# Output projections: squares added up on VectorE before TensorE sums them

## The reference, cut to what matters

```python
def rms_norm(x, gain):
    y = x * lax.rsqrt(jnp.mean(x * x, axis=-1, keepdims=True) + NORM_EPS)
    return y * gain

# first block, after the attention branches
x = x + rms_norm(merged @ w_out, mix_post_norm)

# each of the two layers of the second block
x = x + g1 * (mixed @ w_out_2)
h2 = modulate(rms_norm(x, ffn_norm_g_2), sh2, sc2)
x = x + g2 * hierarchical_moe(h2, ...)     # router, then 32 experts
```

## Time and profile before

| | |
|---|---|
| median of the runs | 1594.91 us |
| the profiled execution, its own time | 1594.11 us |
| its span in the profile | 1592.4 us |
| TensorE busy | 1458.5 us (92%) |
| VectorE busy | 903.3 us (57%) |
| ScalarE busy | 576.6 us (36%) |
| mean TensorE clock granted, share of full | 0.961 |
| read from HBM | 416.71 MB |

### The profile page before, as it was taken

How to read it: one execution, slowest core, us unless ns; L and a number is a source line. 1 busy time by engine, 2 the same in 40 slices (tenths; PEclk the granted TensorE clock), 3 DMA queues, 4 the chain that set the end, 5 groups by cost and what they waited for, 6 DMA issues and landing times.

```text
span 1592.4 us, 27000 instructions
## 1 busy us (share of the span) xinstructions
PE 1458.5 (92%) x10609; PEld 1180.4 (74%) x10609; DVE 903.3 (57%) x1609; ACT 576.6 (36%) x916; POOL 3.7 (0%) x9
## 2 busy tenths in 40 slices
PE   9999999989888899999999999987779999988776
PEld 8999999979787898999989898422217989532223
DVE  6898877684444476888877985210015996410002
ACT  4544356423435544433445153221115143321101
POOL 0000000000000000000000000000000000000000
PEclk9999999999989998999999999999988999999897
DMA  8998844412513353988866558899996749699995
GB/s 304 381 356 306 307 166 154 148 43 107 186 67 107 106 167 138 339 308 305 301 225 220 190 207 323 332 409 409 409 409 234 280 133 373 266 408 409 409 409 222
DMA packets 115804, 420.88 MB, mean 264 GB/s; under 512 B 12944, under 2 KB 13088, under 8 KB 115568
## 3 DMA queue, kind: packets, MB, share of 16 engines
q1 hardware_dynamic: 114624, 414.19, 69.8%
q0 software_dynamic: 1072, 5.20, 0.9%
HBM read 416.71 MB, written 2.62 MB: 263 GB/s over the span
## 4 chain that ended last, share of the span: by engine, by line
PE 68%; DMA 11%; SPq 7%; DVE 6%; ACT 4%; issue 3%; DVEq 0%; ACTq 0%
PE work L930 26%; PE acc L930 12%; PE work L965 7%; SPq L752 7%; PE work L1021 5%; PE work L1566 3%; DMA hf<-wstream_d 3%; PE work L890 2%; PE work L900 2%; DMA over_splits<-wstream_d 2%; ACT whi L1656 2%; PE work L1593 1%; DVE wlo L2106 1%; PE work L1501 1%; DMA over_select<-wstream_d 1%
## 5 line engine op out<-in xcount | busy, mean ns | idle before, releaser
L2106 DVE TENSOR_TENSOR wlo<-raw,whi 128x1024 fp32r<-128x1024 f32 x264 | 320.9, 1222 | 176.6 <-ACT whi L1656 176.0
L1656 ACT ACTIVATE whi<-raw 128x1024 fp32r<-128x1024 f32 x264 | 277.0, 1056 | 280.3 <-PE work L930 191.7
L930 PE MATMUL work<-hhi,whi 128*128 128x256 f32 x1024 | 295.0, 288 | 1.7 <-DVE wlo L2106 0.9
L930 PE MATMUL work<-hlo,whi 128*128 128x256 f32 x1024 | 292.9, 286 | 0.0
L930 PE MATMUL work<-hhi,wlo 128*128 128x256 f32 x1024 | 292.7, 286 | 0.0
L930 PEld LDWEIGHTS work<-hhi,whi 128*128 128x128 f32 x1024 | 200.0, 195 | 3.9 <-DVE wlo L2106 3.0
L930 PEld LDWEIGHTS work<-hlo,whi 128*128 128x128 f32 x1024 | 199.9, 195 | 0.3
L930 PEld LDWEIGHTS work<-hhi,wlo 128*128 128x128 f32 x1024 | 199.7, 195 | 0.0
L2845 DVE TENSOR_TENSOR pair_b<-work,pair_a 128x256 f32<-128x256 f32 x16 | 6.8, 424 | 215.3 <-ACT pair_a L2061 215.3
L2212 DVE SCALAR_TENSOR_TENSOR ada_tiles<-ada_tiles,c_act 128x1024 f32<-128x1024 f32 x96 | 116.3, 1219 | 2.0 <-DMA ada_tiles<-ada_d 2.0
L965 PE MATMUL work<-hf,raw 128*128 128x256 f32 x512 | 111.5, 379 | 0.0
(11 more groups left out here) (482 smaller groups left out, 2708.5 us busy)
## 6 DMA issues: line engine op xcount, KB each, us to landing
raw<-wstream_d SPq DMA_DIRECT2D x376, 512.0 KB, 4.7
ada_tiles<-ada_d SPq DMA_DIRECT2D x96, 512.0 KB, 5.2
over_splits<-wstream_d SPq DMA_DIRECT2D x80, 512.0 KB, 15.3
over_select<-wstream_d SPq DMA_DIRECT2D x48, 512.0 KB, 14.5
over_end<-wstream_d SPq DMA_DIRECT2D x24, 512.0 KB, 14.9
spare_d<-wstream_d SPq DMA_DIRECT2D x24, 512.0 KB, 14.4
over_pool<-wstream_d SPq DMA_DIRECT2D x22, 512.0 KB, 15.2
hf<-wstream_d SPq DMA_DIRECT2D x20, 512.0 KB, 15.0
```

The lines of the kernel that those rows point to most:

```text
L930: mm = pe.matmul(out, a, b, start=(start and k == 0), stop=(stop and k == n - 1), skip_group_check=skip)
L1656: act.activation(whi[n % AHEAD][:], tiles[SLOT[SPLITS[n]]][:], ACT.Copy).then_inc(s("hi_done"), 1)
L2106: dve.tensor_tensor(wlo[n % AHEAD][:], tiles[SLOT[SPLITS[n]]][:], whi[n % AHEAD][:].bitcast(F32), ALU.subtract).then_inc(s("lo_done"), 1)
```

## The change

VectorE adds the squares of pair 1 and then of pair 2 onto those of pair 0, in place in `hf`, each when ScalarE has written them. The second add signals `squares_added`. TensorE leaves out the groups for pair 1 and 2: its group for pair 0 now stands behind tile 7 and waits for `squares_added`; the group for pair 3 stays last. `router_part` stays where it was, and waits for the squares of its pair by itself. In the layers one zero product instead of five stands between the two groups. The three places are the first projection (norm 4) and that of each layer (norms 9 and 12).

```diff
@@ norm_part, TensorE
-            def norm_part(k, j):
+            def norm_part(k, j, added=None):
...
-                pe.wait_ge(s("norm_sq"), NORM_AT[k] + j + 1)
+                if added is None:
+                    pe.wait_ge(s("norm_sq"), NORM_AT[k] + j + 1)
+                else:
+                    pe.wait_ge(s("squares_added"), after("squares_added", added))
@@ router_part, TensorE
+                pe.wait_ge(s("norm_sq"), NORM_AT[9 + 3 * l] + j + 1)
                 if j == 0:
@@ out_tiles, TensorE
-                    if n > 4:
-                        norm_part(k, n - 5)
-                        if layer is not None:
-                            router_part(layer, n - 5)
+                    if n > 4 and layer is not None:
+                        router_part(layer, n - 5)
+                norm_part(k, 0, 1 if layer is None else 2 + layer)
                 hold(1, hold_last)
                 norm_part(k, 3)
@@ the layers' call, TensorE
-                out_tiles(f"wout{l}", "mixed_ready", 4 * l, k + 2, 5, 0, l)
+                out_tiles(f"wout{l}", "mixed_ready", 4 * l, k + 2, 1, 0, l)
@@ VectorE
+            def add_squares(k, j):
+
+                dve.wait_ge(s("norm_sq"), NORM_AT[k] + j + 1)
+                return dve.tensor_tensor(hf[:, 0:2, :], hf[:, 0:2, :], hf[:, 2 * j:2 * j + 2, :], ALU.add)
...
             for m in range(DC - 1):
                 lo(NUMBER[START["wout"] + m] + AHEAD)
+                if m == 5:
+                    own(add_squares(4, 1))
+                elif m == 6:
+                    add_squares(4, 2).then_inc(s("squares_added"), 1)
...
                         residual_pair(m - 4, lambda m: mod_col(l, 2, m))
+                    if m == 5:
+                        own(add_squares(k + 2, 1))
+                    elif m == 6:
+                        add_squares(k + 2, 2).then_inc(s("squares_added"), 1)
```

More of the change, by code:

```diff
@@ L332 @@
     **shared("dn_vector", [(n, 1) for n in ("dn_absz", "dn_decay", "dn_var", "dn_gc", "dn_recip", "dn_rest", "dn_unit",
-                                            "dn_scales", "dn_ovar", "dn_orecip", "dn_scaled", "dn_out")]),
+                                            "dn_scales", "dn_ovar", "dn_orecip", "dn_scaled", "dn_out")]
+             + [("squares_added", 1 + LAYERS)]),
     **shared("first_scalar", [("c_ready", 1), ("mem_squares", 4), ("mem_high", 4)]),
```

## The result

The changed kernel takes 1585.35 us in the median of 8 runs (1582.43 to 1590.12), against 1594.91 for before; the measured ratio is 0.995, 95% interval 0.9935 to 0.9965. That is 8.0 us; by the two medians alone it would be 9.6. Single executions of one kernel differ by 7 to 10 us within a sample, so it matters what in the 7 to 8 us is the change's own.

The account below looks back on a forecast made before the run. It took TensorE's path (68% of the chain) as the bound, with DMA at 18%. From the profiled 1594.11, less 1.07 and 2 x 2.45, plus 1.67 for clock, came 1589.81; adding 0.80 for the median gave 1590.6, range 1588.3 to 1593.1.

Parts of the forecast that it names:

- Sums removed, layers: Each layer's output projection: two groups of sums of 0.79 us go, saving 1.58; with the zero products 2.45.
- Zero products: Between the layers' last sums: five become one, saving 0.87 us a layer, with 0.35 us of slack left.
- First projection: Two groups removed save 1.58 us, less a 0.51 wait for VectorE's add: a gain of 1.07.
- Work in sum: First projection's 1.07 us plus 2.45 in each of two layers: 5.97 saved before any clock cost.
- Expert stages: Transfers start when TensorE frees the first buffer, so a gain ahead of the stage survives as an earlier start.
- The rival falls: Rival: transfer-bound expert stages swallow the layers' gain, leaving only the first projection's 1.07 us; 1593.8, chance 0.10.
- The clock: TensorE's clock falls behind the sums in one of the two layers, costing 1.67 us; chance 0.38.
- rival "slower": Clock lost behind both layers' sums through zero products and gather: 4.11 us a layer plus 0.71; 1597.9, chance 0.04.
- The row of 617 to 618: Profile slice by the first projection's sums: TensorE busy 1.00 while its clock falls, taken as evidence busy time can cost clock.
- the reading that only idleness costs clock: Reading of the skill's clock-gate page: no idle time added in the layers, so no clock cost; sum 1588.95.
- the case without any fall: Rival: no clock is lost in the layers; 1588.9 us, or 1588.2 if layer 0's gather keeps its clock; chance 0.28.

Follow-up runs that it names:

- adds first, one: Changed kernel with VectorE's adds ahead of the splits in the first projection, one zero product per layer kept; ratio 0.995 (0.9935 to 0.9965).
- with none: Changed kernel with no zero product between the two groups of sums in the layers; ratio 0.9972 (0.9957 to 0.9987).
- the second profile of the change: Changed kernel run once more, unaltered, for a second sample of executions; ratio 0.9956 (0.9942 to 0.9969), median 1587.49 us.
- one, alone: Kernel before with one zero product in place of five in each layer, nothing else; ratio 0.9972 (0.9959 to 0.9985).
- layers only: Changed kernel with the first projection put back to four groups of sums, only both layers changed; ratio 0.9988 (0.9974 to 1.0002).

## Why the prediction was wrong, step by step

- *Sums removed, layers.* Right in kind, slightly small. Forecast 2.45 a layer with the zero products, shown 2.66 (12.90 to 10.24): each of the three router groups behind a tile is 0.10 shorter, which no row of before showed, and the sums with the zero product are 0.09 longer.
- *Zero products.* Right: 0.87 a layer (12.90 to 12.03 alone, 11.11 to 10.24 in the change). The cover was as thin as computed: in "adds first, one" the last squares end 0.34 before their sum, where 0.35 was forecast, and with none nothing more is won.
- *First projection.* The mechanism was right: the add behind the split, done at 613.31 against 613.25. Forecast 1.07, shown 0.88 at full clock (12.22 to 11.34) and 0.29 where the clock falls in the sums. The tiles close up by 1.79, not 1.58 (first to last squares 10.42 before, 8.63 now), but the wait is 0.63, not 0.51, and 0.25 of issue and longer groups stand behind it.
- *Work in sum.* Forecast 5.97, shown 0.88 + 2 x 2.66 = 6.20.
- *Expert stages.* The restart moved earlier with TensorE (1000.35 to 993.46), and the end moved by more, so the transfers didn't swallow the gain. The rival falls. The surplus of 5.7 us in these stages was in no term; the second profile of the change has 1.2 of it.
- *The clock.* This is the term that failed. I took the falls of the kernel before as given and added 1.67 for one more. That leaves a gain of 4.3 us with the work as forecast and 4.5 as shown, and both samples exclude either (5.6 to 10.4 and 4.9 to 9.2). Taken over the executions, the clock's net part and all else that is not work is the measured gain less the work: 0.8 in the second sample, 1.8 in the first, where the forecast had -1.67.

Part of the term was right. In each of the two profiles of the change the clock fell behind the sums of one layer of the two, as forecast. The size was between 1.4 (17.85 against 16.44) and 4.5 us (20.90 against 16.43), since the router group (+0.84), transposes (+1.68), zero products (+0.69) and the gather (+1.23) slow down one after another. The rival "slower" had priced that long fall well, at 4.11 and 0.71 for the gather. By the means above, the changed order with one zero product costs 0.6 a layer more than that of before from root to restart, 1.3 in two. So a loss near the forecast one is there in the profiles, and something else makes up for it in the samples. Where it does is open: in the first profile of the change it is mostly the expert stretches, in the second "between", and other profiles of the same code show neither reliably.

The row of 617 to 618, set in the prediction against the reading that only idleness costs clock, was weak for that. In the slice before it TensorE was busy for less than half, in the columns of the earlier trace rows:

```profile
616.00:617.00 1.00, 0.45 (x5) 0.36 (x4) 0.17 (x1) 0.84 (x2) 0.00 (x0) 1.00 0.45 180
```

Layer 1 of the change is the better witness: busy for 0.92 or more of every slice from 1336 on, and the clock fell at 1345.

Whether the net part is above zero isn't settled: 6.2 lies inside both intervals. For "one, alone" (4.5 against 1.7) and "layers only" (1.9 against 5.3) the work lies outside, with opposite signs; two of thirteen is more than one expects of 95% intervals, but not by much. That stretches of the same code differ with the clock is shown for the profiled executions. Whether an edit moves the falls, by the hour or otherwise, or an execution draws them, is not shown: no kernel but the change was profiled twice. The range should have carried a clock term of both signs; it stopped 0.6 below the case without any fall.

## What to carry to other kernels

Where TensorE's clock falls and rises, two executions of the same code differ by more than a small saving is worth, here by 5.4 us ahead of any edit. So read the work from a stretch that holds the change, at equal granted clock, and don't read a gain or a loss from an unchanged stretch of one profile: look at that stretch in other kernels that have the same code there. A delay with nothing saved tests whether a gain depends on the hour, but it needs a sample whose interval is narrower than the delay; 1.1 us against intervals of 2 to 3 us either way didn't decide. And add up the whole span: the stretches that were looked at first summed to nothing, and the surplus stood in one that wasn't.

## What the runs showed that I had not expected

- A high busy share doesn't keep the clock: in layer 1 of the change every slice of a microsecond was busy for 0.92 or more, with a tile, router groups, sums of one column (four of them 0.79 us) and one zero product, and the clock fell from 1.00 to 0.52.
- One fall costs very different amounts by what runs in it: 0.6 us in two groups of sums (1.93 to 2.53), 1.7 in sixteen transposes (1.78 to 3.46), 1.2 in the twelve-row gather (1.70 to 2.93).
- A router group of four products is 0.82 behind a tile of products and 0.92 behind a sum.
- The kernel before with 1.1 us of zero products added was not measurably slower (0.3 us faster, interval from 1.8 slower to 2.4 faster).
- No version was clearly better than the change: the adds ahead of the splits with one zero product gave the same ratio with 0.9 us less work.
